# A token mixer whose attention is laid between the matmuls of its input projection

## The chip, the cores and the metric

The kernel runs on one core of one Trainium2 chip. The metric is the device time of one execution in microseconds (us). TensorE (PE), VectorE (DVE), ScalarE (ACT), GpSimd (POOL) and SyncE (SP) each take their own queue of instructions in order, and wait for one another by semaphores. SP issues nearly all DMAs; its transfers follow one another on one ring.

## The reference

The input is x, 256 tokens of 1024 values in float32. A first block has two layers, and each layer is three stages: a gated feed-forward net (FFN1), a token mixer, and a second feed-forward net (FFN2). Each stage is modulated by rows that come from `cond @ w_ada[l] + b_ada[l]`, and each ends in a layer norm. A second block follows: attention with pooling, experts, a short convolution, and experts again; nothing in it is touched here.

The token mixer is where the change is:

```python
def _token_mixer(h, w_in, w_out):
    proj = h @ w_in                          # 1024 -> 3072 columns
    rq, rk, rv, rg, dq, dk, dv, sq, sk, sv = jnp.split(proj, points, axis=-1)
    y_ret = _retention(_rotate(rq), _rotate(rk), rv, rg)   # silu(g) * group_norm(o)
    y_dil = _dilated_attention(_rotate(dq), _rotate(dk), dv)
    y_sb = _stick_breaking(sq, sk, sv)
    return jnp.concatenate([y_ret, y_dil, y_sb], -1) @ w_out
```

(`_split_heads`, `_merge_heads` and the frequencies are left out.) There are four heads of each of the three kinds. All of them read only their own columns of `proj`.

## The kernel before, in words

**The projection.** The 3072 columns are six groups of 512: group 0 is retention q and k, 1 retention v, 2 the gate g, 3 dilated q and k, 4 dilated v and stick-breaking q, 5 stick-breaking k and v. Each group has two token tiles of 128, so there are twelve products (proj0 to proj11, line 767), each of eight contraction steps into one PSUM bank (4 to 7 in turn). ACT copies each bank into `proj` (line 1186). Groups are computed in the order 0 to 5.

**The attention.** After the twelve products PE transposes q and k of all heads (line 789, six sets of four), ACT and DVE copy them out (lines 1199, 1599), and six blocks of two heads follow, in the order `ATT`: dilated, stick-breaking, dilated, stick-breaking, retention, retention. A block is scores (A, lines 799 to 803), a middle part on DVE and ACT, a second PE step (B, lines 813 to 819; not for retention) and the product with the values (C, lines 839 to 841). PE runs two blocks in turn, in banks 4 and 5, and 6 and 7. The gate goes through Silu on ACT (line 1191) ahead of the attention. At the end DVE norms the retention output (lines 1702 to 1714), multiplies it by the gate (line 1718), PE turns y (line 669), and the output projection runs (line 744), first token tile, then second; norm and modulation of the next stage follow on DVE and ACT.

**The modulation rows.** Beside this the kernel computes the rows that later stages need. In the mixer these are five rows a layer, each from a 1024 by 1024 matrix that SP streams into two buffers (`W_mod`) in four chunks of 1 MB (line 407). A chunk's transfer is issued only when DVE has used the chunk two before it. DVE multiplies and adds the chunks (`mod_blocks`, lines 1375 and 1377, eight instructions a row), PE sums over the partitions (`mod_sum`, line 656), DVE adds the bias (line 1391), ACT sends the row to DRAM (line 1088). PE takes the five sums between the products: behind proj2, 4, 6, 8 and 11. DVE takes the rows in one piece each, with the two rotations (lines 1560 to 1566) between them.

**The order of SP's ring.** `MIX_CHUNKS` says ahead of which weight slot which chunks are issued. Weights of `w_in` (slots u = 0 to 11, 1 MB each, line 477), then `w_out` (four of 1 MB), then the first weights of FFN2 follow in the same ring, behind the chunks that stand ahead of them.

All these orders are written out by hand; no planner sets them.

Of the kernel before, what the change touches and what calls it, by code (L numbers as in the profile page):

```python
# [22 lines left out]
P = 128  # L23
S = 256
# [36 lines left out]
MIX_SUMS = (2, 4, 6, 8, 11)  # L61
MIX_CHUNKS = {2: (0, 2), 6: (2, 10), 8: (10, 14), 10: (14, 18), 12: (18, 20)}
# [79 lines left out]
def build(nc, A, out):  # L142
    with ExitStack() as ctx:
# [6 lines left out]
        def steps(name, names):  # L150
            return Steps(sem(name), names)
# [30 lines left out]
        mix_acc = [mod_acc, att_0]  # L182
# [28 lines left out]
        def carve(at, *shape):  # L211
# [116 lines left out]
        m_pe = steps("mixer_pe", [f"proj{n}" for n in range(12)] + [f"qk{g}" for g in range(6)] + ["A0", "A1"]  # L328
                     + sum([([f"B{b}"] if b < 4 else []) + [f"C{b}"] + ([f"A{b + 2}"] if b < 4 else [])
                            for b in range(6)], []) + ["out"])  # L330
        m_act = steps("mixer_act", [f"ev{n}" for n in range(12)] + ["silu_g", "qk0", "qk2", "qk4", "exp0", "ln1",
                                    "PT0", "exp2", "a1", "PT2", "ln3", "a3", "gn_sqrt"])
        m_dve = steps("mixer_dve", ["rot0", "rot1", "qk1", "qk3", "qk5", "max0", "na1", "p0", "lk1", "max2", "y0",
                                    "s1", "am1", "p2", "na3", "y1", "lk3", "y2", "s3", "r4", "am3", "r5", "y3",
                                    "gn_var", "y"])
# [46 lines left out]
        def _(sp):  # L382
# [55 lines left out]
            def ffn_stream(l, k):  # L438
# [4 lines left out]
                if k == 1:  # L443
                    sp.wait_ge(m_pe.s, m_pe.at("out", l))
# [7 lines left out]
            for l in range(LAYERS):  # L452
# [5 lines left out]
                for u in range(MIX_USES):  # L458
# [3 lines left out]
                    if u < 2:  # L462
                        sp.wait_ge(pn_x, l * 6 + 2)
                    elif u < 6:
                        sp.wait_ge(pe_down, l * (2 * TILES) + (1 + TILES))
                    elif s >= 6:
                        last = u - 6 if u < MIX_IN_USES else s
                        sp.wait_ge(m_pe.s, m_pe.at(f"proj{2 * (last // 2) + 1}", l))
                    if u < MIX_IN_USES:
                        g, half = u // 2, u % 2  # L470
# [73 lines left out]
        def _(pool):  # L544
# [85 lines left out]
        def _(pe):  # L630
# [104 lines left out]
            def times_rows(src, slots):  # L735

                at = []
                for tt in range(TT):
# [8 lines left out]
                    if tt == 0:  # L747
                        ins.then_inc(acc_t0, 1)
                return ins

            def mixer(l):
# [7 lines left out]
                for g in range(6):  # L759
                    for t in range(TT):  # L760
                        n = 2 * g + t
                        if n >= 4:
                            pe.wait_ge(m_act.s, m_act.at(f"ev{n - 4}", l))
                        for kc in range(KC):
                            u = 2 * g + kc // 4
                            s = slot(u) if kc % 4 == 0 else MIX_S[u]
                            ins = pe.matmul(psum[:, 4 + n % 4, :], uT[:, kc, P * t:P * t + P],  # L767
                                            part(W[:, s, :], 0, 4, 512)[:, kc % 4, :], start=(kc == 0), stop=(kc == KC - 1))
                        ins.then_inc(m_pe.sig(f"proj{n}"), 1)
                        if n in MIX_SUMS:  # L770
                            row = MIX_SUMS.index(n)
                            mod_sum(l * JOBS_LAYER + (FIRST_JOBS + PAIRS + row), 0, mix_acc[row % 2])

                for g in range(6):
                    kind, hb = g // 2, g % 2
                    if g < 4:
                        pe.wait_ge(m_act.s, m_act.at(f"ev{8 + g}", l))
                    if g == 0:
                        pe.wait_ge(m_dve.s, m_dve.at("rot0", l))
                    if g == 2:  # L780
                        pe.wait_ge(m_dve.s, m_dve.at("rot1", l))
                    if g == 4:
                        pe.wait_ge(m_act.s, m_act.at("qk0", l))
                        pe.wait_ge(m_act.s, m_act.at("ev11", l))
                    if g == 5:
                        pe.wait_ge(m_dve.s, m_dve.at("qk1", l))
                    for n, col in enumerate((QCOL[kind], KCOL[kind])):
                        for t in range(TT):
                            ins = pe.transpose(psum[:, 4 + g % 4, S * n + P * t:S * n + P * t + P],
# [54 lines left out]
                for g in (2, 4):  # L844
                    pe.wait_ge(m_act.s, m_act.at(f"qk{g}", l))
                pe.wait_ge(m_dve.s, m_dve.at("qk5", l))
                scores(0)
                scores(1)
                for b in range(6):
                    if b < 4:  # L850
                        second(b)
                    if b == 4:
                        pe.wait_ge(mod_taken, l * JOBS_LAYER + (FIRST_JOBS + 2 * PAIRS))
                    if b == 2:
                        pe.wait_ge(m_dve.s, m_dve.at("y0", l))
                    if b == 3:
                        pe.wait_ge(m_dve.s, m_dve.at("y1", l))
                    values(b)
                    if b < 4:
                        if ATT[b][0] == STB:  # L860
                            pe.wait_ge(m_dve.s, m_dve.at(f"s{b}", l))
                        scores(b + 2)
# [219 lines left out]
        def _(act):  # L1082
# [100 lines left out]
            def mixer(l):  # L1183
                for n in range(12):
                    act.wait_ge(m_pe.s, m_pe.at(f"proj{n}", l))
                    act.activation(proj[:, n % 2, 512 * (n // 2):512 * (n // 2) + 512], psum[:, 4 + n % 4, :], copy
                                   ).then_inc(m_act.sig(f"ev{n}"), 1)
                    if n in (5, 7, 9):
                        mod_row(l * JOBS_LAYER + (FIRST_JOBS + PAIRS + (n - 5) // 2))
                act.drain()  # L1190
                act.activation(proj[:, :, RG:RG + 512], proj[:, :, RG:RG + 512], ACT.Silu).then_inc(m_act.sig("silu_g"), 1)
                mod_row(l * JOBS_LAYER + (FIRST_JOBS + PAIRS + 3))
                for g in (0, 2, 4):
                    kind, hb = g // 2, g % 2
                    bk = psum[:, 4 + g % 4, :]
# [5 lines left out]
                mod_row(l * JOBS_LAYER + (FIRST_JOBS + PAIRS + 4))  # L1201
# [23 lines left out]

                exps(0)
                logs(1)
                p_turned(0)
                exps(2)
                stick(1)  # L1230
                p_turned(2)
                logs(3)
                stick(3)
                act.wait_ge(m_dve.s, m_dve.at("gn_var", l))
# [731 lines left out]
```

## Time and profile before

| | us |
|---|---|
| median of 3 runs | 2592.54 (2589.14 to 2592.95) |
| the profiled execution, its own time | 2593.06 |
| its span, first to last instruction | 2591.2 |
| PE busy in the span | 2089.6 (81%) |
| DVE busy | 1119.6 (43%) |
| ACT busy | 526.0 (20%) |
| mixer of layer 0, first projection matmul to the turning of y | 251.44 to 410.89 |
| mixer of layer 1, the same | 873.01 to 1031.23 |

A time in the trace is the start of an instruction or of a merged run of them, in us from the start of the span. Of two figures at a row's head the second is how long it lasts.

### The profile page before, as it was taken

What the parts mean: (1) busy time and instruction counts of PE and PEld (TensorE: products, weight loads), DVE (VectorE), ACT (ScalarE), POOL (GpSimd) and SP (SyncE); (2) the same over time, 40 slices, a digit from 0 to 9 for tenths busy, and PEclk for the clock granted to TensorE, in tenths of its full rate; (3) what the DMA queues carried; (4) which work ended last, traced back from release to release, by engine and by line L of the source; (5) the groups of instructions that cost most, each with busy time, mean ns of one, the idle gap of its engine ahead of it and who ended that gap; (6) DMA issues with size and microseconds to landing.
All of it is one profiled execution on the core that took longest, in us unless ns stands there. A gap on an engine that the chain in (4) does not pass through costs nothing.

```text
span 2591.2 us, 33380 instructions
## 1 busy us (share of the span) xinstructions
PE 2089.6 (81%) x12372; PEld 1323.1 (51%) x12372; DVE 1119.6 (43%) x1724; ACT 526.0 (20%) x858; POOL 66.1 (3%) x96
## 2 busy tenths in 40 slices
PE   6998977999799885899978777777769876666664
PEld 4997344999799434599855422222228542111111
DVE  3887554888788665688633310000022331000002
ACT  3332031433334104233323100000010110000000
POOL 1000000000000000000100000000000000000000
PEclk7998987999899898899989787777769978888887
DMA  9986851888588691588721699999995469999996
GB/s 333 327 308 221 290 210 55 281 316 314 201 296 298 212 355 50 187 297 318 268 108 66 235 410 410 410 410 410 410 386 176 167 247 409 410 410 410 410 410 262
DMA packets 289371, 758.03 MB, mean 293 GB/s; under 512 B 17616, under 2 KB 125424, under 8 KB 289184
## 3 DMA queue, kind: packets, MB, share of 16 engines
q1 hardware_dynamic: 282368, 737.34, 75.7%
q0 software_dynamic: 6688, 19.78, 2.4%
q8 instruction: 36, 0.59, 0.1%
q14 instruction: 23, 0.19, 0.0%
q10 hardware_dynamic: 256, 0.13, 0.0%
HBM read 756.01 MB, written 1.18 MB: 292 GB/s over the span
## 4 chain that ended last, share of the span: by engine, by line
PE 51%; DMA 21%; SPq 13%; DVE 8%; issue 3%; ACT 3%; DVEq 1%; ACTq 0%
PE psum L704 20%; DMA W<-in_w_exp_up 15%; SPq L502 12%; PE psum L716 9%; PE psum L744 4%; DMA W_mod<-in_mod_w 4%; PE psum L1071 3%; PE psum L1010 3%; PE psum L767 2%; DMA W<-in_w_exp_down 1%; PE psum L912 1%; PE psum L677 1%; ACT uT L1117 1%; SPq L506 1%; DVE att L1377 1%
## 5 line engine op out<-in xcount | busy, mean ns | idle before, releaser
L704 PE MATMUL psum<-parts 128*128 128x256 f32 x4224 | 528.3, 286 | 14.8 <-DVE parts L1501 7.5
L704 PEld LDWEIGHTS psum<-parts 128*128 128x128 f32 x4224 | 525.8, 195 | 22.4 <-issue 16.2
L1010 PE MATMUL psum<-W,scr 128*32 128x512 f32 x2048 | 316.9, 730 | 151.4 <-DMA W<-in_w_exp_up 136.4
L1877 DVE TENSOR_TENSOR scr<-scr,psum 128x256 f32<-128x256 f32 x32 | 13.5, 421 | 572.4 <-ACT scr L1327 572.4
L1377 DVE SCALAR_TENSOR_TENSOR mod_acc<-W_mod,cond,mod_acc 128x1024 f32<-128x1024 f32 x182 | 233.8, 1285 | 60.1 <-DMA W_mod<-in_mod_w 29.2
L716 PE MATMUL psum<-parts 128*128 128x512 f32 x1056 | 257.8, 393 | 0.0
L1010 PEld LDWEIGHTS psum<-W,scr 128*32 128x32 f32 x2048 | 53.7, 118 | 393.1 <-DMA W<-in_w_exp_up 306.8
L1035 PE MATMUL psum<-W,scr 128*32 128x256 f32 x2048 | 181.3, 498 | 68.3 <-DMA W<-in_w_exp_down 53.2
L1501 DVE TENSOR_TENSOR parts<-W,parts 128x1024 fp32r<-128x1024 f32 x176 | 207.1, 1220 | 56.9 <-ACT parts L1147 56.7
L716 PEld LDWEIGHTS psum<-parts 128*128 128x128 f32 x1056 | 192.6, 188 | 45.3 <-DVE parts L1514 8.2
L1147 ACT ACTIVATE parts<-W 128x1024 fp32r<-128x1024 f32 x176 | 175.7, 1051 | 46.4 <-issue 46.4
L767 PE MATMUL psum<-W,uT 128*128 128x512 f32 x384 | 176.2, 619 | 5.1 <-DVE uT L1421 3.3
L1047 PE MATMUL psum<-scr 128*128 128x512 f32 x256 | 141.8, 704 | 31.9 <-DVE scr L1890 29.8
L1035 PEld LDWEIGHTS psum<-W,scr 128*32 128x32 f32 x2048 | 69.3, 136 | 174.9 <-DMA W<-in_w_exp_down 103.1
L1890 DVE COPY scr<-psum 32x256 f32<-32x256 f32 x64 | 27.2, 426 | 254.8 <-PE psum L1035 254.3
L1327 ACT ACTIVATE scr<-psum 128x256 f32<-128x256 f32 x32 | 12.3, 383 | 603.6 <-PE psum L1010 603.6
L767 PEld LDWEIGHTS psum<-W,uT 128*128 128x128 f32 x384 | 75.3, 199 | 102.4 <-issue 102.4
L1514 DVE TENSOR_TENSOR parts<-W,parts 128x1024 fp32r<-128x1024 f32 x88 | 107.3, 1219 | 10.3 <-ACT parts L1159 10.3
L1166 ACT ACTIVATE att<-psum 128x256 f32<-128x256 f32 x88 | 33.8, 384 | 380.5 <-PE psum L704 380.5
L1047 PEld LDWEIGHTS psum<-scr 128*128 128x128 f32 x256 | 55.0, 227 | 107.6 <-issue 60.4
L1159 ACT ACTIVATE parts<-W 128x1024 fp32r<-128x1024 f32 x88 | 92.9, 1056 | 43.1 <-PE psum L716 43.1
L677 PE MATMUL psum<-k_ident,x_tok 128*128 128x128 f32 x160 | 35.4, 396 | 66.7 <-DVE x_tok L1485 62.2
(283 smaller groups left out, 1744.1 us busy)
## 6 DMA issues: line engine op xcount, KB each, us to landing
W<-in_w_exp_down SPq DMA_DIRECT2D x128, 1024.0 KB
W<-in_w_exp_gate SPq DMA_DIRECT2D x256, 512.0 KB, 14.3
W<-in_w_exp_up SPq DMA_DIRECT2D x256, 512.0 KB, 15.7
W_mod<-in_mod_w SPq DMA_DIRECT2D x123, 1024.0 KB, 6.0
W<-in_ffn_w_gate SPq DMA_DIRECT2D x44, 1024.0 KB, 9.6
W<-in_ffn_w_up SPq DMA_DIRECT2D x44, 1024.0 KB, 12.0
W<-in_ffn_w_down SPq DMA_DIRECT2D x44, 1024.0 KB, 9.3
W<-in_w_in SPq DMA_DIRECT2D x24, 1024.0 KB, 8.5
```

What stands on the lines that cost most here:

```text
L502: sp.dma_start(W[:, s, D * n:D * n + D], w[layer, ds(e, 1), P * s:P * s + P, :] .rearrange("a p n -> p (a n)")).then_inc(landed[s], 16)
L704: ins = pe.matmul(psum[:, 4 + t % 2, S * g:S * g + S], w[:, t % 2, g, kc, :], u[:, kc, :], start=(n == 0 and kc == 0), stop=(n == 2 and kc ...
L716: ins = pe.matmul(psum[:, 2 * tt + h, :], h_[:, t % 2, P * tt:P * tt + P], w[:, t % 2, 512 * h:512 * h + 512], start=(t == 0 and n == 0), ...
L744: ins = pe.matmul(psum[:, 2 * tt + h, :], src[:, kc, P * tt:P * tt + P], w[:, kc % 2, 512 * h:512 * h + 512], start=(kc == 0), stop=(kc == ...
L767: ins = pe.matmul(psum[:, 4 + n % 4, :], uT[:, kc, P * t:P * t + P], part(W[:, s, :], 0, 4, 512)[:, kc % 4, :], start=(kc == 0), stop=(kc ...
L1010: ins = pe.matmul(psum[32 * q:32 * q + 32, 4, :].rearrange("p (g n) -> p g n", g=2), xe_now[:, kc, :], w[:, :, q, :], start=(kc == 0), sto ...
L1035: ins = pe.matmul(psum[32 * q:32 * q + 32, 6, 0:256], e_hT[:, c % 2, 32 * (c // 2):32 * (c // 2) + 32], part(W[:, s, :], 0, 2, D)[:, c % 2 ...
L1047: ins = pe.matmul(psum[:, 2 * tt + h, :], GT[:, P * tt:P * tt + P], R[:, 512 * h:512 * h + 512], start=first, stop=True, skip_group_check= ...
L1147: ins = act.activation(gu_hi[:, t % 2, g, :, :], part(W[:, b + g, :], 0, KC, STEP)[:, :, P * (t % 2):P * (t % 2) + P], copy)
L1377: ins = dve.scalar_tensor_tensor(acc[:, :], w, col, acc[:, :], mul, add)
L1501: ins = dve.tensor_tensor(gu_lo[:, t % 2, g, :, :], part(W[:, b + g, :], 0, KC, STEP)[:, :, P * (t % 2):P * (t % 2) + P], gu_hi[:, t % 2, ...
L1514: dve.tensor_tensor(d_lo[:, t % 2, :], part(W[:, b + 2, :], 0, 2, D)[:, t % 2, :], d_hi[:, t % 2, :].bitcast(F32), sub).then_inc(lo_d, 1)
```

## The change

The order of the groups becomes 3, 4, 5, 0, 1, 2. The products are now called p30, p31, p40 and so on (group, token tile), and the attention's steps stand between them in PE's queue. ACT's and DVE's queues are written in an order that follows. Further:

- Row 3 of the modulation is cut in four pairs of blocks between the attention's steps on DVE; row 4 is computed behind the turning of y, its PE sum stands between the two token tiles of the output projection (a new hook in `times_rows`), its last two chunks are issued with FFN2's stream, and its last steps on DVE (`mixer_row(l, 4)`) and ACT stand in the next norm.
- `MIX_CHUNKS` puts fewer chunks ahead of each weight slot.
- The rotations use `gate_row` as scratch; POOL's load of `gate_row` therefore waits for the second rotation (`rot0`), and the loads behind it in POOL's queue too.
- Probabilities of the dilated heads are turned into columns of the gate (`RG`), and the gate's own product for the second token tile (p21) and the Silu come behind the attention.

The diff, cut to its core:

```diff
-MIX_SUMS = (2, 4, 6, 8, 11)
-MIX_CHUNKS = {2: (0, 2), 6: (2, 10), 8: (10, 14), 10: (14, 18), 12: (18, 20)}
+MIX_GROUPS = (3, 4, 5, 0, 1, 2)
+MIX_BANK = (3, 3, 3, 1, 6)
+MIX_CHUNKS = {2: (0, 2), 6: (2, 8), 8: (8, 12), 10: (12, 16), 12: (16, 18)}
-        mix_acc = [mod_acc, att_0]
+        mix_acc = [mod_acc, att_0, mod_acc, mod_acc, mod_acc]
-        dil_pT = proj[:, :, 0:3 * P]
+        dil_pT = proj[:, :, RG:RG + 3 * P]
-        rope_a, rope_b = tmp[:, 0, 0:512], tmp[:, 1, 0:512]
+        rope_a, rope_b = gate_row[:, 0:512], gate_row[:, 512:1024]
@@ SP, ffn_stream
                 if k == 1:
+                    for c in (2, 3):
+                        mod_chunk(l * JOBS_LAYER + (FIRST_JOBS + 2 * PAIRS - 1), c, PAIRS - 1)
                     sp.wait_ge(m_pe.s, m_pe.at("out", l))
@@ SP, w_in
-                        sp.wait_ge(m_pe.s, m_pe.at(f"proj{2 * (last // 2) + 1}", l))
+                        sp.wait_ge(m_pe.s, m_pe.at(f"p{MIX_GROUPS[last // 2]}1", l))
@@ POOL, gate
+                if s in (1, 4):
+                    pool.wait_ge(m_dve.s, m_dve.at("rot0", s // 3))
@@ PE, times_rows
                     if tt == 0:
                         ins.then_inc(acc_t0, 1)
+                        between()
@@ PE, mixer
+                project(3, 0, 4)
+                project(3, 1, 5)
+                project(4, 0, 6)
+                row_sum(0)
+                project(4, 1, 7)
+                pe.wait_ge(m_act.s, m_act.at("ev30", l))
+                project(5, 0, 4)
+                row_sum(1)
+                pe.wait_ge(m_act.s, m_act.at("ev40", l))
+                pe.wait_ge(m_dve.s, m_dve.at("rot1", l))
+                heads_turned(2, 6)
+                pe.wait_ge(m_act.s, m_act.at("ev31", l))
+                project(5, 1, 5)
+                pe.wait_ge(m_act.s, m_act.at("ev41", l))
+                heads_turned(3, 7)
+                project(0, 0, 0)
+                row_sum(2)
+                pe.wait_ge(m_act.s, m_act.at("ev51", l))
+                heads_turned(4, 6)
+                pe.wait_ge(m_dve.s, m_dve.at("qk3", l))
+                heads_turned(5, 7)
+                scores(0)
+                project(0, 1, 1)
...
+                scores(1)
+                second(0)
...
+                project(1, 0, 0)
+                values(0)
+                scores(2)
+                second(1)
...
+                project(1, 1, 1)
...
+                values(1)
+                scores(3)
+                second(2)
...
+                project(2, 0, 0)
+                pe.wait_ge(m_dve.s, m_dve.at("y0", l))
+                values(2)
+                pe.wait_ge(m_dve.s, m_dve.at("rot0", l))
+                heads_turned(0, 4)
+                heads_turned(1, 5)
...
+                row_sum(3)
+                second(3)
...
+                scores(4)
...
+                values(3)
+                scores(5)
...
+                values(4)
+                values(5)
+                project(2, 1, 4)
                 turn(y_tok, lambda t: (m_dve.s, m_dve.at("y", l)))
                 turned(l * 4 + 2)
-                times_rows(uT, lambda u: slot(MIX_IN_USES + u)).then_inc(m_pe.sig("out"), 1)
+                times_rows(uT, lambda u: slot(MIX_IN_USES + u), lambda: row_sum(4)).then_inc(m_pe.sig("out"), 1)
@@ ACT, mixer (its end)
+                evacuate(2, 0, 0)
+                heads(0, 4)
                 stick(3)
+                row_out(3)
                 act.wait_ge(m_dve.s, m_dve.at("gn_var", l))
                 act.activation(rstd[:, :], rstd[:, :], ACT.Sqrt).then_inc(m_act.sig("gn_sqrt"), 1)
+                evacuate(2, 1, 4)
+                act.drain()
+                act.activation(proj[:, :, RG:RG + 512], proj[:, :, RG:RG + 512], ACT.Silu).then_inc(m_act.sig("silu_g"), 1)
                 turn(l * 4 + 2)
@@ DVE, mixer
+                mixer_blocks(0)
+                rotated(1, DIL, 3)
+                mixer_blocks(1)
+                mixer_row(l, 0)
+                mixer_blocks(2)
+                mixer_row(l, 1)
+                heads(3, 7)
+                mixer_blocks(3, 0, 2)
+                mixer_row(l, 2)
+                heads(5, 7)
                 maxima(0)
+                mixer_blocks(3, 2, 4)
+                weighted(0)
                 neg_abs(1)
-                weighted(0)
+                rotated(0, RET, 0)
                 keeps(1)
+                mixer_blocks(3, 4, 6)
                 maxima(2)
+                sticks(1)
                 dil_out(0)
-                sticks(1)
                 stick_mask(1)
                 weighted(2)
+                stick_out(1)
                 neg_abs(3)
-                stick_out(1)
+                mixer_blocks(3, 6, 8)
                 keeps(3)
                 dil_out(2)
+                heads(1, 5)
+                mixer_row(l, 3)
                 sticks(3)
                 decayed(4)
                 stick_mask(3)
...
                 turn(l * 4 + 2)
+                mixer_blocks(4)
@@ DVE, between the mixer and its norm
                 plus_bias(s + 1)
+                mixer_row(l, 4)
```

## Rows read from the trace of the kernel before

**Rows 1.** The chain that ended last, from the page: by engine, by line.

```profile
PE 51%; DMA 21%; SPq 13%; DVE 8%; issue 3%; ACT 3%; DVEq 1%; ACTq 0%
PE psum L704 20%; DMA W<-in_w_exp_up 15%; SPq L502 12%; PE psum L716 9%; PE psum L744 4%; DMA W_mod<-in_mod_w 4%; PE psum L1071 3%; PE psum L1010 3%; PE psum L767 2%; DMA W<-in_w_exp_down 1%; PE psum L912 1%; PE psum L677 1%; ACT uT L1117 1%; SPq L506 1%; DVE att L1377 1%
```

**Rows 2.** Timeline of PE, layer 0's mixer: start, us, line, what, count, idle before.

```profile
251.44 23.91 PE L767 MATMUL psum<-W,uT 128*128 128x512 f32 x48 [1.67 <-DVE uT L1421]
...
291.24 14.00 PE L767 MATMUL psum<-W,uT 128*128 128x512 f32 x32
...
325.61 0.88 PE L656 MATMUL psum<-att,k_ones 128*32 128x256 f32 x8 [3.90 <-DVE mod_out L1391]
326.42 22.27 PE L767 MATMUL psum<-W,uT 128*128 128x512 f32 x48
348.63 0.64 PE L656 MATMUL psum<-mod_acc,k_ones 128*32 128x256 f32 x8
349.20 1.97 PE L789 MATMUL psum<-k_ident,scr 128*128 128x128 f32 x16
...
362.19 0.88 PE L813 MATMUL psum<-k_ident,att 128*128 128x128 f32 x6 [3.91 <-DVE att L1624]
...
403.27 0.39 PE L841 MATMUL psum<-scr,tmp 128*128 128x128 f32 x2
410.89 3.68 PE L669 MATMUL psum<-k_ident,tmp 128*128 128x128 f32 x16 [7.24 <-DVE tmp L1718]
415.46 27.70 PE L744 MATMUL psum<-W,uT 128*128 128x512 f32 x64 [0.90 <-issue]
```

**Rows 3.** Windows: stretch, length, busy us of five engines, granted clock, DMA.

```profile
290.00:349.00 59.00, 52.70 (x144) 22.22 (x144) 34.84 (x39) 4.33 (x8) 3.53 (x4) 0.97 0.95 348
349.00:362.00 13.00, 6.11 (x48) 5.07 (x40) 8.89 (x23) 9.42 (x19) 0.00 (x0) 1.00 0.82 284
362.00:404.00 42.00, 28.22 (x132) 24.01 (x132) 18.68 (x48) 13.75 (x16) 0.00 (x0) 0.72 0.00 0
```

**Rows 4.** Timeline of PE, layer 1's mixer: beginning, end of the projection, turning of y.

```profile
873.01 23.73 PE L767 MATMUL psum<-W,uT 128*128 128x512 f32 x48 [1.66 <-DVE uT L1421]
...
970.64 1.97 PE L789 MATMUL psum<-k_ident,scr 128*128 128x128 f32 x16
...
1031.23 3.68 PE L669 MATMUL psum<-k_ident,tmp 128*128 128x128 f32 x16 [7.41 <-DVE tmp L1718]
```

**Rows 5.** Timeline of DVE, layer 0: modulation rows, first softmax, the next norm.

```profile
299.09 5.38 DVE L1377 SCALAR_TENSOR_TENSOR mod_acc<-W_mod,cond,mod_acc 128x1024 f32<-128x1024 f32 x4 [3.81 <-DMA W_mod<-in_mod_w]
304.39 0.42 DVE L1391 TENSOR_TENSOR mod_out<-psum,cond_now 128x256 f32<-128x256 f32 x1
...
357.01 0.42 DVE L1612 SCALAR_TENSOR_TENSOR att<-psum,k_closed 128x256 f32<-128x256 f32 x1 [1.40 <-PE psum L800]
...
429.47 1.23 DVE L1462 TENSOR_TENSOR tmp<-psum,gate_row 128x1024 f32<-128x1024 f32 x1 [5.91 <-PE psum L744]
...
443.21 1.23 DVE L1462 TENSOR_TENSOR tmp<-psum,gate_row 128x1024 f32<-128x1024 f32 x1 [9.34 <-PE psum L744]
```

**Rows 6.** Timeline of SP: DMA issues, layer 0's mixer.

```profile
286.07 1.02 SPq L477 DMA_DIRECT2D W<-in_w_in  x2
...
304.91 1.08 SPq L477 DMA_DIRECT2D W<-in_w_in  x2
```

**Rows 7.** DMA issues of 236 to 456 us: KB each, us to landing.

```profile
W_mod<-in_mod_w SPq DMA_DIRECT2D x20, 1024.0 KB, 6.2
W<-in_w_in SPq DMA_DIRECT2D x10, 1024.0 KB, 8.8
```

**Rows 8.** Timeline of ACT: the gate's Silu in layer 0.

```profile
348.73 0.60 ACT L1186 ACTIVATE scr<-psum 128x512 f32<-128x512 f32 x1 [6.27 <-PE psum L767]
349.39 1.28 ACT L1191 ACT_TABLE_LOAD   x1
350.69 1.06 ACT L1191 ACTIVATE scr<-scr 128x1024 f32<-128x1024 f32 x1
```

More of the change, by code:

```diff
@@ L326, in build @@
         s_out = sem("out_stored")
[L328 to L335, printed above, removed]
+        m_pe = steps("mixer_pe", "p30 p31 p40 p41 p50 qk2 p51 qk3 p00 qk4 qk5 A0 p01 A1 B0 p10 C0 A2 B1 p11 C1 A3 B2 p20 C2 "
+                     "qk0 qk1 B3 A4 C3 A5 C4 C5 p21 out".split())
+        m_act = steps("mixer_act", "ev30 ev31 ev40 ev41 ev50 qk2 ev51 ev00 qk4 exp0 ev01 ln1 PT0 ev10 exp2 a1 ev11 PT2 ln3 "
+                      "ev20 qk0 a3 gn_sqrt ev21 silu_g".split())
+        m_dve = steps("mixer_dve", "rot1 qk3 qk5 max0 p0 na1 rot0 lk1 max2 s1 y0 am1 p2 y1 na3 lk3 y2 qk1 s3 r4 am3 r5 y3 "
+                      "gn_var y".split())
         P2 = [f"c{t}" for t in range(TT)] + [f"p{t}{g}" for t in range(TT) for g in range(3)]
@@ L733, in ffn, with times_rows @@
                 pe.wait_ge(mod_taken, l * JOBS_LAYER + (FIRST_JOBS + PAIRS + 2 * PAIRS * k))
-            def times_rows(src, slots):
+            def times_rows(src, slots, between=lambda: None):
                 at = []
@@ L756, in slot @@
                     return s
[L759 to L772, printed above, removed]
@@ L774, in mixer, with project @@
-                for g in range(6):
-                    kind, hb = g // 2, g % 2
[L776 to L786, printed above, removed]
+                def project(g, t, bank):
+                    for kc in range(KC):
+                        u = 2 * MIX_GROUPS.index(g) + kc // 4
+                        s = slot(u) if kc % 4 == 0 else MIX_S[u]
+                        ins = pe.matmul(psum[:, bank, :], uT[:, kc, P * t:P * t + P],
+                                        part(W[:, s, :], 0, 4, 512)[:, kc % 4, :], start=(kc == 0), stop=(kc == KC - 1))
+                    ins.then_inc(m_pe.sig(f"p{g}{t}"), 1)
@@ L846, in mixer @@
+                pe.wait_ge(m_act.s, m_act.at("qk4", l))
                 pe.wait_ge(m_dve.s, m_dve.at("qk5", l))
-                scores(0)
                 scores(1)
[L849 to L862, printed above, removed]
+                second(0)
@@ L1183, in mixer, with evacuate, row_out, heads @@
             def mixer(l):
[L1184 to L1193, printed above, removed]
+                def evacuate(g, t, bank):
+                    act.wait_ge(m_pe.s, m_pe.at(f"p{g}{t}", l))
+                    act.activation(proj[:, t, 512 * g:512 * g + 512], psum[:, bank, :], copy).then_inc(m_act.sig(f"ev{g}{t}"), 1)
+                def row_out(n):
+                    mod_row(l * JOBS_LAYER + (FIRST_JOBS + PAIRS + n))
+                def heads(g, bank):
                     kind, hb = g // 2, g % 2
-                    bk = psum[:, 4 + g % 4, :]
+                    bk = psum[:, bank, :]
                     act.wait_ge(m_pe.s, m_pe.at(f"qk{g}", l))
@@ L1567, in rotate, with mixer_row, mixer_blocks, heads @@
                 ins.then_inc(m_dve.sig(f"rot{table}"), 1)
+            def mixer_row(l, n):
+                job = l * JOBS_LAYER + (FIRST_JOBS + PAIRS + n)
+                mod_row(job, (pe_mod, job - FIRST_JOBS + 2), MIX_BANK[n], None, mix_bias[n % 2], 2 * l + (n + 1) // 2)
             def mixer(l):
-                def mixer_blocks(n):
+                def mixer_blocks(n, first=0, end=KC):
                     job = l * JOBS_LAYER + (FIRST_JOBS + PAIRS + n)
-                    mod_blocks(job, job - FIRST_JOBS - (1 if n else 0), 0, KC, mix_acc[n % 2])
-                def mixer_row(n):
-                    job = l * JOBS_LAYER + (FIRST_JOBS + PAIRS + n)
-                    mod_row(job, (pe_mod, job - FIRST_JOBS + 2), 0, None, mix_bias[n % 2], 2 * l + (n + 1) // 2)
+                    mod_blocks(job, job - FIRST_JOBS - (1 if n in (1, 2) else 0), first, end, mix_acc[n])
                 def rotated(table, kind, group):
                     dve.drain()
-                    dve.wait_ge(m_act.s, m_act.at(f"ev{2 * group + 1}", l))
+                    dve.wait_ge(m_act.s, m_act.at(f"ev{group}1", l))
                     rotate(l, kind, table)
-                mixer_blocks(0)
-                mixer_blocks(1)
-                rotated(0, RET, 0)
-                mixer_row(0)
-                mixer_blocks(2)
-                mixer_row(1)
-                mixer_blocks(3)
-                mixer_row(2)
-                rotated(1, DIL, 3)
-                mixer_blocks(4)
-                mixer_row(3)
-                for g in (1, 3, 5):
+                def heads(g, bank):
                     kind, hb = g // 2, g % 2
-                    bk = psum[:, 4 + g % 4, :]
+                    bk = psum[:, bank, :]
                     dve.wait_ge(m_pe.s, m_pe.at(f"qk{g}", l))
```

38 lines of the change are left out of this document (32 added, 6 removed).

## The prediction

> **What bounds the kernel now.** I read the chain that ended last first [rows 1]: TensorE holds 51% of it, and the DMAs that hold 21% and most of SP's 13% belong to the experts' weights, which the change does not touch. The feed-forward nets around each mixer are lines 704 and 716, 29% of the chain, so a mixer that ends earlier moves all that follows it by the same amount. Then PE's timeline in layer 0's mixer [rows 2]. The twelve products run from 251.44 to 349.20, nearly without a gap. The attention follows to 403.66. The norm of the retention heads and the gate's multiplication take until 410.89, where y is turned; the output projection starts at 415.46. The reader is to see two unlike halves in the windows [rows 3]. From 290 to 349 PE is busy 52.70 of 59 us and ACT 4.33. From 349 to 404 PE is busy 6.11 + 28.22 of 55 us, and the second part of that runs at a granted clock of 0.72. PE waits there for short steps of DVE and ACT that hang on one another. Layer 1 has the same form, 873.01 to 1031.23 [rows 4]: 158.2 us against 159.5.
>
> **What a product costs.** 32 records of line 767 last from 291.24 to 305.17, two products, so 6.9 us each [rows 2]. The first three took 23.91 us where 3 x 6.9 = 20.7: 3.2 us lost to the low clock at the start. The attention's own PE work at full clock is 6.11 x 1.00 + 28.22 x 0.72 = 26.4 us [rows 3], the turning of q and k included. A row's sum costs 0.6 us [rows 2].
>
> **PE's new queue, layer 0.** Up to the last values (C5) it holds eleven products, 75.9 us; the slow start, 3.2; four sums, 2.4; the attention, 26.4. That is 107.9 us. Nothing of the arithmetic goes; what goes is the idle time of the attention, into which seven products (p51 to p21) are laid. Before, the same point was reached after 403.66 - 251.44 = 152.2 us.
>
> **The waits that stay.** First, the third row's sum. PE gets there after seven products, two sums, the slow start and two sets of turned heads (1.0): 53.7 us, at 305.1. DVE had the second row done at 304.8 before [rows 5], paced by `W_mod`: a chunk lands 6.2 us after its issue [rows 7] and is issued only when DVE has used the one two before. In the new ring two slots of w_in (2 MB) pass ahead of chunks 8 and 9, where they came behind them at 286.07 [rows 6]; at the ring's 348 to 400 GB/s that is 2.6 us a MB, half of it hidden behind the two-chunk loop, so row 2 is ready near 307.5. The rotation stays one, in another gap. Wait: 2.4 us, between 0 and 5. Second, the first dilated block. Chunk 12 lands behind slots 8 and 9 of w_in, near 312 (before, these slots came at 304.91, behind chunk 13). Behind it DVE does two blocks (2.6), a row (0.4), a head group (1.3, three copies of the size of line 1391's), the maxima, two more blocks (2.6) and the weighting. From the start of the maxima to B0 it was 5.2 us before (357.01 to 362.19 [rows 2, 5]), of which 1.9 is the stick-breaking step that now comes later; so B0 is free near 312 + 4.3 + 3.3 + 2.6 = 322.2. PE is there at 319: 307.5 plus a sum, two sets of heads, a product and two scores. Wait: 3.2 us, between 0 and 6. Third, the values of block 3: two decay products and two mask products on DVE, 0.42 for 256 columns [rows 5], about 2 us with nothing of PE's ahead. All other steps of DVE and ACT lie beside a product of 6.9 us, which is longer than the logarithms' chain with its table load. These three waits are 7.6 us. A gap also costs clock: behind a wait of 3.90 us a sum took 0.88 and three products 22.27 instead of 20.7 [rows 2], 1.6 to 1.8 us. I take 2.5 for gaps of this size, between 0 and 5. C5 ends after 107.9 + 7.6 + 2.5 = 118.0 us.
>
> **The end of the mixer.** Before, 7.2 us stood between C5 and the turning [rows 2]. Now the product p21 is behind C5 (6.9), and the gate comes behind it: the copy 0.60, the table load 1.28, the Silu 1.06 [rows 8], the multiplication 1.23 (the size of line 1462's [rows 5]), with 0.3 between them: 11.4 us. The norm of the retention heads hides under p21. The Silu was free before, beside the turning of q and k; here it is the last link. The copy needs no table of its own, and the load stood right behind the copy in the row, 0.06 us after it, so I do not let it start before p21.
>
> Here a rule of the Trainium skill and the row differ. In the row the Silu starts 0.02 us after the load's 1.28 have passed [rows 8]. The Trainium skill (ScalarE: Activation LUTs, What ACT_TABLE_LOAD costs) adds a drain of about 1.38 us to every switch, 2.66 in all. By that the two layers together would be 2.8 us later. The measured row decides, and the sum goes without it.
>
> **The sum.** y is turned after 118.0 + 11.4 = 129.4 us instead of 159.5: 30.1 us less in layer 0. In layer 1, 158.2 - 129.4 = 28.8. Off this comes the output projection's added sum, 0.6 a layer. Row 4 now starts on DVE only behind the turning of y. Its eight blocks take 10 us, and its last two chunks (issue to landing 6.2 us [rows 7]) bring it to about 13.8; the first token tile ends 14.0 us after the projection's start (415.46 to 429.47 [rows 2, 5]). So PE just does not wait, or up to 3 us if a chunk takes the 8.8 us of w_in [rows 7]. DVE then has two splits of gate and up weights, the bias, the row and the first half of the norm, 13 us, and is free at 27; the second half of the norm was late on PE at 27.8 (443.21). The cover is about one us thick; I take 0.3 a layer. POOL's load of gate_row and the columns behind it come some 70 us later than before and are needed only in the next norm, 100 us further on: nothing. w_out is issued behind chunk 17, near 348, and lands by 366; it is needed at 382: nothing. Together 30.1 + 28.8 - 1.2 - 0.6 = 57.1. Against the profiled execution's own 2593.06 this gives 2535.9; that run stands 0.5 above the median of 2592.54. I say 2535.
>
> **The range.** With none of the waits and no clock loss each layer gives 10.1 more: 2515. With the waits at their upper ends (5, 6, 4), 5 of clock and 3 in the output projection, 13 less: 2561. For eight in ten I take 2516 to 2553.
>
> **Rivals.** (a) DVE and the `W_mod` loop set the pace. For it: DVE was busy 62.4 of the 114 us from 290 to 404 [rows 3], and the same work, less row 4's 10 us, must fit a stretch 34 us shorter, in a strict order with blocks that wait for DMA (3.81 us before one group [rows 5]). Against it: after chunk 13 every block has its data long before its turn. If each of the seven interleaved steps waited 3 us, 21 instead of 7.6, two layers would give 27 less: 2562. Chance 0.10. (b) The clock stays low in the whole interleaved stretch. For it: 0.72 in 362 to 404, where PE worked in short pieces [rows 3]. Against it: 0.97 from 290 to 349 with gaps up to 3.90 us. Place: p51 to p21 with the attention, 7 x 6.9 + 26.4 = 74.7 us at full clock. At the lower of the two levels, 1.2 of 2.4 GHz, it costs 74.7 a layer against 29 gained: 2593 + 2 x 46 = 2685. It turns to slower where the mean clock is under 74.7 / (74.7 + 29) = 0.72. Chance 0.03. The Trainium skill (TensorE: Matmul & The Clock Gate, A second HAM failure mode: psum-queue depth-cycling) speaks against this change: short pauses between groups of matmuls can make the clock swing between its two levels. The gap rows show that only in part, 1.7 us behind a gap of 3.90. (c) The gain is won and mostly given back in the output stage, because row 4 is late: chunks 18 and 19 queue behind FFN2's first 3 MB, and norm and PE slip by 8 us a layer: 2551. Those 3 MB should be in before; chance 0.05. (d) The change does not do what it says, a wait in PE's queue (the count of `mod_taken`, or `ev` of a late bank) holds the products until the old times: 2593. PE's order makes that unlikely; 0.02. The forecast itself has 0.80.
>
> A measurement here tells 0.2%, 5 us, from no change. All of (a), (c) and the forecast are faster by more; so faster is 0.95; same is (d), 0.02; slower is (b), 0.03.
>
> **What would show it.** In the trace after: y turned near 129 us after the first product; the idle time before the third sum, before B0 and before block 3's values 2 to 3 us each; granted clock above 0.9 from 290 to 370; the table load of the Silu behind the copy of p21 and 4 to 5 us of idle PE there; the sum of row 4 without idle before it, and the second half of the norm still released by PE. A clock near 0.7, or DVE waiting for `W_mod` behind chunk 13, or more than 15 us of idle PE between the first product and C5, would make it wrong.

## The result, and the profile after

The changed kernel takes 2526.37 us (median of 4 runs, 2524.13 to 2532.63) beside 2590.84 for the kernel before on the same chip (2588.03 to 2592.95, 4 runs). The ratio is 0.9756, 95% interval 0.9735 to 0.9777: 2.4% faster. Predicted were 2535.0, between 2516 and 2553. The profiled execution took 2525.63, its span is 2523.8 (before: 2591.2), so 67.4 us less.

The page after, the chain that ended last, by engine and by line (answers to [rows 1]):

```profile
PE 54%; DMA 21%; SPq 13%; DVE 6%; issue 3%; ACT 2%; DVEq 1%; ACTq 0%
PE psum L707 20%; DMA W<-in_w_exp_up 16%; SPq L503 12%; PE psum L719 9%; PE psum L747 5%; PE psum L768 4%; PE psum L1103 3%; DMA W_mod<-in_mod_w 3%; PE psum L1042 3%; DMA W<-in_w_exp_down 1%; PE psum L944 1%; PE psum L680 1%; SPq L507 1%; ACT uT L1149 1%; PE psum L1054 1%
```

The shares of the experts' weights are nearly as they were. PE has more of the chain, DVE and ACT less, and the products (now line 768) went from 2% to 4%: they bridge what was a chain through DVE and ACT.

PE's timeline in layer 0's mixer after, the first products, the rows with a wait, the products that stand between steps, and the turning of y (answers to [rows 2]):

```profile
249.58 23.40 PE L768 MATMUL psum<-W,uT 128*128 128x512 f32 x48 [1.66 <-DVE uT L1476]
...
304.24 0.64 PE L659 MATMUL psum<-mod_acc,k_ones 128*32 128x256 f32 x8 [1.42 <-DVE mod_out L1446]
...
307.15 7.03 PE L768 MATMUL psum<-W,uT 128*128 128x512 f32 x16
...
318.69 0.87 PE L805 MATMUL psum<-k_ident,att 128*128 128x128 f32 x6 [3.20 <-DVE att L1668]
319.40 8.73 PE L768 MATMUL psum<-W,uT 128*128 128x512 f32 x16
...
332.35 7.03 PE L768 MATMUL psum<-W,uT 128*128 128x512 f32 x16
...
342.52 7.03 PE L768 MATMUL psum<-W,uT 128*128 128x512 f32 x16
...
357.39 0.41 PE L831 MATMUL psum<-scr,tmp 128*128 128x64 f32 x2 [1.87 <-DVE tmp L1693]
...
362.84 7.03 PE L768 MATMUL psum<-W,uT 128*128 128x512 f32 x16
374.23 3.60 PE L672 MATMUL psum<-k_ident,tmp 128*128 128x128 f32 x16 [4.36 <-DVE tmp L1778]
```

From 307 on four products stand 10 to 13 us apart, with steps of the attention between them, and p21, the last product, starts at 362.84. From the first product to C5 only three gaps are left in front of PE: the third row's sum, the first dilated block's turning (B0), the values of block 3 (C3). All other steps of the attention find their input ready. Layer 1 begins and its y is turned here (answers to [rows 4]):

```profile
836.18 23.64 PE L768 MATMUL psum<-W,uT 128*128 128x512 f32 x48 [1.66 <-DVE uT L1476]
...
961.82 3.36 PE L672 MATMUL psum<-k_ident,tmp 128*128 128x128 f32 x16 [4.36 <-DVE tmp L1778]
```

The mixer, from its first product to the turning of y, is 124.65 us in layer 0 (before 159.45) and 125.64 in layer 1 (before 158.22): 34.8 + 32.6 = 67.4 us. That is all of the span's gain. Of the other stretches, the one before layer 0's mixer is 1.9 shorter, the one between the mixers 0.2 shorter, and the one behind layer 1's turning 2.0 longer.

The windows of the same places after, columns as in [rows 3]: 290 to 349, then 290 to 363 (C5), then up to the turning:

```profile
290.00:349.00 59.00, 54.38 (x189) 29.26 (x188) 43.96 (x77) 17.93 (x27) 4.05 (x5) 0.97 0.62 218
290.00:363.00 73.00, 66.51 (x278) 39.68 (x277) 51.49 (x96) 22.96 (x34) 4.05 (x5) 0.98 0.70 254
363.00:374.00 11.00, 6.87 (x16) 2.69 (x15) 6.39 (x27) 3.15 (x4) 0.00 (x0) 1.00 0.68 232
```

ACT is busy 17.93 us from 290 to 349 where it was 4.33, and the stretch at a clock of 0.72 [rows 3] is gone: 0.98 up to C5.

### The profile page after: what moved, and what is told of

Read it like the earlier page. It is cut to its first block, busy times and chain, and to the rows that moved or that the text cites. A ratio compares the mean times of both kernels' runs of the same rounds, so it can differ in the third digit from the quotient of the medians.

```text
span 2523.8 us, 33380 instructions
## 1 busy us (share of the span) xinstructions
PE 2078.4 (82%) x12372; PEld 1309.9 (52%) x12372; DVE 1118.6 (44%) x1724; ACT 528.9 (21%) x860; POOL 65.2 (3%) x96
## 4 chain that ended last, share of the span: by engine, by line
PE 54%; DMA 21%; SPq 13%; DVE 6%; issue 3%; ACT 2%; DVEq 1%; ACTq 0%
PE psum L707 20%; DMA W<-in_w_exp_up 16%; SPq L503 12%; PE psum L719 9%; PE psum L747 5%; PE psum L768 4%; PE psum L1103 3%; DMA W_mod<-in_mod_w 3%; PE psum L1042 3%; DMA W<-in_w_exp_down 1%; PE psum L944 1%; PE psum L680 1%; SPq L507 1%; ACT uT L1149 1%; PE psum L1054 1%
## 5 line engine op out<-in xcount | busy, mean ns | idle before, releaser
L1042 PE MATMUL psum<-W,scr 128*32 128x512 f32 x2048 | 323.7, 743 | 136.3 <-DMA W<-in_w_exp_up 122.9
L1432 DVE SCALAR_TENSOR_TENSOR mod_acc<-W_mod,cond,mod_acc 128x1024 f32<-128x1024 f32 x196 | 251.8, 1284 | 51.6 <-issue 28.2
L1556 DVE TENSOR_TENSOR parts<-W,parts 128x1024 fp32r<-128x1024 f32 x176 | 207.0, 1219 | 56.1 <-ACT parts L1179 56.1
L1067 PE MATMUL psum<-W,scr 128*32 128x256 f32 x2048 | 165.8, 463 | 73.6 <-DMA W<-in_w_exp_down 58.5
L1079 PE MATMUL psum<-scr 128*128 128x512 f32 x256 | 160.1, 782 | 31.7 <-DVE scr L1952 29.7
L768 PE MATMUL psum<-W,uT 128*128 128x512 f32 x384 | 176.6, 617 | 3.3 <-DVE uT L1476 3.3
L1079 PEld LDWEIGHTS psum<-scr 128*128 128x128 f32 x256 | 63.3, 262 | 117.7 <-issue 70.3
L1569 DVE TENSOR_TENSOR parts<-W,parts 128x1024 fp32r<-128x1024 f32 x88 | 107.2, 1218 | 10.3 <-ACT parts L1191 10.3
L747 PE MATMUL psum<-W,uT 128*128 128x512 f32 x192 | 86.6, 611 | 2.7 <-issue 1.9
```

Of the source, the lines that this page charges most:

```text
L747: ins = pe.matmul(psum[:, 2 * tt + h, :], src[:, kc, P * tt:P * tt + P], w[:, kc % 2, 512 * h:512 * h + 512], start=(kc == 0), stop=(kc == ...
L768: ins = pe.matmul(psum[:, bank, :], uT[:, kc, P * t:P * t + P], part(W[:, s, :], 0, 4, 512)[:, kc % 4, :], start=(kc == 0), stop=(kc == KC ...
L1042: ins = pe.matmul(psum[32 * q:32 * q + 32, 4, :].rearrange("p (g n) -> p g n", g=2), xe_now[:, kc, :], w[:, :, q, :], start=(kc == 0), sto ...
L1067: ins = pe.matmul(psum[32 * q:32 * q + 32, 6, 0:256], e_hT[:, c % 2, 32 * (c // 2):32 * (c // 2) + 32], part(W[:, s, :], 0, 2, D)[:, c % 2 ...
L1079: ins = pe.matmul(psum[:, 2 * tt + h, :], GT[:, P * tt:P * tt + P], R[:, 512 * h:512 * h + 512], start=first, stop=True, skip_group_check= ...
L1432: ins = dve.scalar_tensor_tensor(acc[:, :], w, col, acc[:, :], mul, add)
```

## Experiments

All ratios are to the kernel before, run on the same chip; "mixer" is first product to turning of y, layer 0 / layer 1, in the profiled execution.

**1. The attention behind all products.** Order of the column groups, rows and ring (but one chunk) as changed; only the interleaving is undone, on PE and in ACT's copies.

```diff
- ... qk5 A0 p01 A1 B0 p10 C0 A2 B1 p11 C1 A3 B2 p20 C2 qk0 qk1 B3 A4 C3 A5 C4 C5 p21
+ ... qk5 p01 p10 p11 p20 p21 A0 A1 B0 C0 A2 B1 C1 A3 B2 C2 qk0 qk1 B3 A4 C3 A5 C4 C5
```

> The changed kernel with its order of groups, its rows and its rings, but the attention again behind all twelve products: p01, p10, p11, p20 and p21 stand ahead of the first scores (the last two stay in banks 0 and 1 until the second dilated block is done, and the ring gives slots 10 and 11 one chunk earlier). Theory (the gain is idle time of the attention that the products fill): the first scores begin 5 x 6.9 = 34 us later than after, and from them to the last values it takes the 48 us of before, plus up to 5 us for the row's blocks that DVE has between; the end of the mixer is 7 us again, since the gate is ready. So 22 to 30 us more a layer: 2570 to 2586, idle PE of about 20 us back in each attention, granted clock there near 0.75. Rival (the order of the groups and the modulation rows moved behind bring it): at most 10 us a layer more, 2546 or less.

Measured: 2573.43 us, ratio 0.9919 [0.9901, 0.9936]; mixer 151.63 / 152.02, 27.0 and 26.4 above the changed kernel, inside the 22 to 30 expected. Windows of its products' second half and of its attention:

```profile
308.00:341.60 33.60, 33.60 (x82) 14.95 (x81) 3.54 (x6) 3.95 (x7) 0.00 (x0) 1.00 0.41 154
342.50:396.00 53.50, 35.27 (x165) 29.48 (x163) 36.65 (x78) 18.03 (x26) 4.06 (x5) 0.71 0.51 176
```

The two unlike halves are back: first PE alone at full clock, then DVE busy 36.65 of 53.50 us and a clock of 0.71. So the interleaving itself is worth 53.4 of the 67.4 us, in the mixers of the profiled executions; the medians of this run and the changed kernel are 47.1 us apart. PE's marked waits inside the mixer add up to 27.0 us in layer 0 here and to 10.9 in the changed kernel, so 16.1 of the 27.0 us are idle time. Nearly all of the other 10.9 is the same matmuls at a lower clock: two scores of line 794 take 0.59 us at 343.72 and 1.17 at 369.65. The other 7.8 us of layer 0 are mostly in the products' stretch. It ran 97.8 us before (251.44 to 349.20 [rows 2]) and 91.0 here. Before, it held waits of 0.83, 1.73 (for `w_in`) and 3.90 us; here it holds one of 1.52:

```profile
306.47 0.64 PE L659 MATMUL psum<-mod_acc,k_ones 128*32 128x256 f32 x8 [1.52 <-DVE mod_out L1441]
308.07 34.50 PE L768 MATMUL psum<-W,uT 128*128 128x512 f32 x80
```

**2. Only the late sum, in the kernel before.** It asks whether that 3.90 us wait alone could have been moved away.

```diff
-MIX_SUMS = (2, 4, 6, 8, 11)
+MIX_SUMS = (2, 4, 6, 9, 11)
```

> The kernel before with one number changed: PE's sum of the fourth row stands behind proj9 instead of proj8, so that PE does not wait for DVE there (3.9 and 4.0 us before, and some 1.7 us of low clock behind the wait in layer 0). Theory (PE's queue bounds the projection, so a wait in it is time in full): 8 to 11 us less, 2580 to 2583. Rival (the chunk loop of the rows bounds the projection, and the wait only moves to the fifth sum): no change, 2588 to 2593.

Measured: 2599.08 us, ratio 1.0017 [1.0005, 1.0028]; mixer 160.58 / 161.70. My theory fell; the rival's number, no change, is right, though the fifth sum does not wait either. The fourth sum waits no more, but PE now reaches the next weights before they are there:

```profile
327.41 0.64 PE L656 MATMUL psum<-att,k_ones 128*32 128x256 f32 x8
331.81 16.77 PE L767 MATMUL psum<-W,uT 128*128 128x512 f32 x32 [3.77 <-DMA W<-in_w_in]
```

Those weights are issued behind a chunk that waits for DVE. The wait changed its name from DVE to DMA, and did not shrink (3.77 us in layer 0 and 5.05 in layer 1, where the sum had waited 3.90 and 4.00): what had to change was the order of the ring and of DVE, not the place of the sum.

**3. Another order of the ring.** Two chunks of row 2 ahead of the weights of the first retention group, as two slots of weights passing ahead of them had been priced at 2.6 us a MB.

```diff
-MIX_CHUNKS = {2: (0, 2), 6: (2, 8), 8: (8, 12), 10: (12, 16), 12: (16, 18)}
+MIX_CHUNKS = {2: (0, 2), 6: (2, 10), 8: (10, 14), 10: (14, 16), 12: (16, 18)}
```

> The changed kernel with another order of SP's ring: chunks 8 and 9 ahead of slots 6 and 7 of w_in, chunks 12 and 13 ahead of slots 8 and 9. Theory (the waits before the third sum, 1.4 and 1.1 us, and before the first B, 3.2 and 4.2 us, come from chunks 8 and 12 that land behind 2 MB of w_in): both waits fall under 1 us, and the product behind B0 takes 6.9 instead of 8.6 us: 5 to 6 us less a layer, 2514 to 2517. Rival (DVE's two blocks between the maxima and the weighting hold B0, not the chunk): 2 us less a layer, 2522. Rival on the other side (w_in is late for p00 or p10 instead): same or slower, 2526 or more.

Measured: 2519.64 us, ratio 0.9721 [0.9700, 0.9741]; mixer 121.80 / 122.25, so 2.85 and 3.4 less, between the theory (5 to 6) and the first rival (2). Its waits and what follows them:

```profile
316.19 0.87 PE L805 MATMUL psum<-k_ident,att 128*128 128x128 f32 x6 [0.98 <-DVE att L1668]
316.90 7.03 PE L768 MATMUL psum<-W,uT 128*128 128x512 f32 x16
...
353.21 0.41 PE L831 MATMUL psum<-scr,tmp 128*128 128x64 f32 x2 [1.87 <-DVE tmp L1693]
...
354.65 1.17 PE L794 MATMUL psum<-qm,scr 128*128 128x256 f32 x2
355.61 0.64 PE L795 MATMUL psum<-qm,scr 128*128 128x128 f32 x2
```

The sum's wait went down by 0.78 and B0's by 2.22, and the product behind B0 is back at 7.03, another 1.7. That would be 4.7. But behind C3's unchanged gap of 1.87 the scores now take 1.17 and 0.64, where after the change they took 0.65 and 0.38, and C3 to the last product takes 7.06 us instead of 5.45. The clock's dip was not removed: it moved, and 1.6 us came back. That is the part of the theory that failed: it had the waits nearly right and counted the dip as gone.

**4. The gate ahead of the last product.** Half of the gate (token tile 0) and the table load are taken before the product p21 is waited for; tile 1 goes through Silu straight from PSUM, and DVE multiplies tile by tile.

```diff
-                evacuate(2, 1, 4)
                 act.drain()
-                act.activation(proj[:, :, RG:RG + 512], proj[:, :, RG:RG + 512], ACT.Silu)...
+                act.activation(proj[:, 0, RG:RG + 512], proj[:, 0, RG:RG + 512], ACT.Silu)...
+                act.wait_ge(m_pe.s, m_pe.at("p21", l))
+                act.activation(proj[:, 1, RG:RG + 512], psum[:, 4, :], ACT.Silu)...
```

> The changed kernel with the gate's end shortened: the Silu of the first token tile, with the table load, stands before p21 is awaited, the second token tile goes through Silu straight from PSUM, and DVE multiplies tile by tile. Theory (after p21 the copy, the table load, the Silu and the multiplication hang on one another, 4.3 us in all): 1.4 us are left, so 2.9 us less a layer, 2520 to 2521. Rival (the norm of the retention heads ends just as late, or a table load costs a drain besides): less than 1 us a layer, 2525 or more.

Measured: 2513.61 us, ratio 0.9687 [0.9667, 0.9708]; mixer 121.74 / 121.97, 2.9 and 3.7 less. ACT's timeline, then the turning of y on PE:

```profile
366.35 1.28 ACT L1288 ACT_TABLE_LOAD   x1
367.64 0.63 ACT L1288 ACTIVATE scr<-scr 128x512 f32<-128x512 f32 x1
370.27 0.60 ACT L1290 ACTIVATE scr<-psum 128x512 f32<-128x512 f32 x1 [2.00 <-PE psum L768]
```

```profile
371.64 1.97 PE L672 MATMUL psum<-k_ident,tmp 128*128 128x128 f32 x16 [1.41 <-DVE tmp L1781]
```

PE's gap fell from 4.36 to 1.41 as expected. The total is 6.4 to 7.4 us below the expectation, and a third of that has a reason that I had not put in. After the change the turning's 16 matmuls ran for 3.60 us behind the gap of 4.36 (3.36 in layer 1); here, behind 1.41, they take 1.97. From the turning to the next net's first matmul it is 43.46 / 43.12 us instead of 44.53 / 44.41, so 2.4 us in all. Layer 1's mixer gives 0.8 beyond the expectation, and there B0's gap is 3.27 instead of 4.22, which the gate does not explain. Where the other 3 to 4 us come from stays open.

**5. Both together, and the changed kernel again.** The edits are those of 3 and 4.

> The changed kernel with both repairs at once: the ring's chunks and weights in the order of the run with the new ring (row chunks 8 and 9 ahead of the weights of the first retention column group), and the gate's Silu and its table load ahead of the last product. The ring's repair took 2.9 and 3.4 us a layer from the mixer (first product to the turning of y) in the stretch up to 350, the gate's 2.9 and 3.7 in the tail, with another 1 us in the output stage: they lie in different places, so theory: they add up, mixer 118.5 to 119.5 a layer against 124.65 and 125.64, span 13 to 17 us below that of the changed kernel, ratio 0.962 to 0.965 of the kernel before. Rival: the tail's gain came from a clock that stays at full speed over the turning of y, and one of the two is used up: then 2512 to 2515, ratio 0.968.

> The changed kernel itself, unaltered, beside the others on the same chip, so that they can be compared with it directly. Ratio to the kernel before 0.974 to 0.978; mixer 124 to 126 us a layer.

Measured: both 2512.67 us, ratio 0.9688 [0.9674, 0.9703], mixer 118.80 / 119.16. The changed kernel 2525.40, ratio 0.9743 [0.9727, 0.9759], mixer 124.49 / 125.29. In the mixer the gains add up as expected: 5.7 and 6.1 a layer below the repetition of the changed kernel. The turning of y takes 1.96 / 1.97 us as in experiment 4, so the rival's cause, a gain that is used up twice, is not seen, although the total lies where the rival put it. The ratio that I expected (0.962 to 0.965) was missed because it did not fit the rest of my expectation: 13 to 17 us below the changed kernel is a ratio of 0.968 to 0.971. Against the repetition on the same chip the medians differ by 12.7 us and the mixers by 11.8, so nothing is missing. What is not told apart from this is the total of experiment 4, 12.8 us below the changed kernel with only 6.6 in its mixers. The profiled execution of both repairs was its fastest, 2505.52, the others took 2510 to 2514. From layer 1's turning of y to the end the profiles of these kernels differ by up to 8 us without a system (1554.3 here, 1562.0 after the change, 1558.5 in its repetition, 1561.1 in experiment 3), and a sum of mixer gains below that size is seen in the mixer only.

**6. The last idle gap filled.** On top of both repairs, the scores A5 stand ahead of C3 on PE, and on DVE the copy behind C3 ahead of the decay of block 5.

```diff
- ... A4 C3 A5 C4 C5 p21        DVE: ... r4 am3 r5 y3
+ ... A4 A5 C3 C4 C5 p21        DVE: ... r4 am3 y3 r5
```

> As the run before it in this list (both repairs), and in addition the scores of the second retention pair of heads ahead of the values of the second stick-breaking pair on TensorE (they wait for the sum that VectorE took of the other pair instead), and on VectorE the copy of the stick-breaking values ahead of the second decay. The idle 1.87 us of TensorE ahead of the values is then filled by scores of 1.3 us, but VectorE's decay comes one copy (some 0.4 us) and one wait later. Theory: 0.3 to 1.3 us a layer less than with both repairs, no more. Rival: the chain from VectorE's mask through values, copy and decay to the last values is as long as what it replaces, and nothing is left (within 0.3 us a layer).

Measured: 2504.51 us, ratio 0.9654 [0.9637, 0.9671]; mixer 116.36 / 116.90, 2.4 and 2.3 less than with both repairs, twice what was expected. PE's timeline:

```profile
353.29 0.60 PE L794 MATMUL psum<-qm,scr 128*128 128x256 f32 x2
353.73 0.38 PE L795 MATMUL psum<-qm,scr 128*128 128x128 f32 x2
354.58 0.43 PE L831 MATMUL psum<-scr,tmp 128*128 128x64 f32 x2 [0.47 <-DVE tmp L1694]
```

The gap is 0.47 instead of 1.87, and the granted clock from 308 to 359 is 1.00:

```profile
308.00:359.00 51.00, 49.57 (x224) 31.49 (x223) 39.55 (x84) 20.73 (x29) 4.06 (x5) 1.00 0.74 274
```

So 1.4 us is the gap and 1.3 the dip, which is seen in neither layer now (C3 to p21 takes 4.44 us, and 7.10 with the scores of 1.31 in it before); 0.3 is lost ahead of it. This version beats both kernels: 3.5% below before, and its interval lies wholly below that of the changed kernel.

**7. Two products fewer between the steps.** In the changed kernel, p01 and p10 stand ahead of the first scores (and their copies ahead on ACT), so that only p11 and p20 are left inside, and p21 in the tail.

```diff
- ... qk5 A0 p01 A1 B0 p10 C0 A2 B1 p11 C1 A3 B2 p20 C2 ...
+ ... qk5 p01 p10 A0 A1 B0 p11 C0 A2 B1 p20 C1 A3 B2 C2 ...
```

> The changed kernel with the attention begun two products later: the second product of group 0 and the first of group 1 stand ahead of the first scores, and three of the five products are left between steps of the attention (the last one stays in the tail). Theory: a product between two steps is worth the wait of VectorE that it covers and the clock that it keeps. Without a product between the first scores and the turning of the first dilated weights, that wait grows from 3.2 us to 8 to 10, and the third dilated step loses its cover as well (some 3 us more), each with a slow product behind it: 8 to 13 us a layer more than the changed kernel, 2542 to 2554. Rival: three products are cover enough, since VectorE is less loaded later on, and the loss is 2 to 4 us a layer: 2530 to 2535.

Measured: 2548.73 us, ratio 0.9833 [0.9814, 0.9852]; mixer 135.95 / 136.20, 11.3 and 10.6 more. The size is as expected, the places only in part:

```profile
329.51 1.54 PE L805 MATMUL psum<-k_ident,att 128*128 128x128 f32 x6 [4.77 <-DVE att L1668]
330.85 7.94 PE L768 MATMUL psum<-W,uT 128*128 128x512 f32 x16
...
360.80 1.65 PE L810 MATMUL psum<-scr,k_later 128*128 128x384 f32 x2 [2.57 <-DVE scr L1693]
```

B0's wait grew to 4.77 (5.12 in layer 1), not to 8: DVE had worked ahead beside the two products and waited for PE's scores before the maxima:

```profile
323.48 0.42 DVE L1656 SCALAR_TENSOR_TENSOR att<-psum,k_closed 128x256 f32<-128x256 f32 x1 [8.31 <-PE psum L792]
```

The rest came late, at the second stick-breaking block (2.57) and behind it, where its large matmuls take 1.65 instead of 0.91 in experiment 6. The clock from 350 to 372 is 0.80, and 1.00 in the changed kernel. In layer 0 PE's waits add up to 6.0 us more than in the changed kernel; the other 5.3 of the 11.3 are nearly all the same matmuls at the lower clock.

## Why the prediction was right, point by point

- **Place and sign.** All of the 67.4 us are in the two mixers, and experiment 1 gives 53.4 of them to the interleaving. Rival (d) is out. The sum of 57.1 is 10.3 short of the span's gain: 8.5 in the two mixers, and 1.8 that I took off for the output stage and that did not come. The mechanism held; most of the errors of size point the same way, so the number was not saved by errors that cancel.
- **PE's queue up to C5.** 107.9 us of work were counted. C5 ended 113.4 after the first product, not 118.0. Of the 4.6, waits are 1.1, the clock's loss 0.8, the slow start 0.5. The rest, 2.2, is the **mis-sized term**: the attention's work, 26.4. What C5's time leaves for it, 113.4 - 75.9 - 2.4 - 2.7 (slow start, 23.40 - 3 x 6.9) - 6.5 (waits) - 1.7 (clock) = 24.2 us. Adding up the attention's rows of the new timeline from start to start, where they run at or near full clock, gives 24.2 as well. I had multiplied PE's busy time by the granted clock [rows 3]. That this came out 2.2 too high may lie in the records, whose ends are modelled and overlap, or in the clock, which is a mean over idle time too; no run separates the two. The product's 6.9 us holds: single ones take 6.87 from start to start, though the pair that I read it from takes 6.97 each.
- **The waits.** The third sum 1.42 / 1.14 (forecast 2.4), B0 3.20 / 4.22 (3.2), C3 1.87 / 1.87 (2.0). This mixer starts 1.9 us earlier than the one before, so its times are compared from the first product: row 2 was done on DVE after 54.5 us (at 304.1), not 56.1, and PE came after 53.2, not 53.7. The chain before B0 came out by its parts, 9.6 us from the chunk's landing to B0 for 10.2 forecast; DVE's first wait there is for the chunk that was named, chunk 12, which lands 59.5 us after the first product (at 309.1), not 60.6:

```profile
309.10 0.75 DVE L1430 TENSOR_SCALAR mod_acc<-W_mod,cond 128x1024 f32<-128x1024 f32 x1 [3.81 <-DMA W_mod<-in_mod_w]
```

- **Clock behind gaps.** One product of 8.73 / 8.44 instead of 7.03, so 1.7 / 1.4 us for 2.5 forecast; in layer 1 the turning at B0 ahead of it loses another 0.3.
- **The tail.** From the end of C5 to the turning 11.2 us for 11.4, link by link: copy, table load, Silu, multiplication (answers to [rows 8]):

```profile
369.90 0.60 ACT L1219 ACTIVATE scr<-psum 128x512 f32<-128x512 f32 x1 [3.98 <-PE psum L768]
370.57 1.28 ACT L1289 ACT_TABLE_LOAD   x1
371.86 1.06 ACT L1289 ACTIVATE scr<-scr 128x1024 f32<-128x1024 f32 x1
```

```profile
372.95 1.23 DVE L1778 TENSOR_TENSOR tmp<-tmp,scr 128x1024 f32<-128x1024 f32 x1 [4.07 <-ACT scr L1289]
```

Here the load is on the path that sets the end, and Silu starts 0.01 us behind its 1.28. The drain that the Trainium skill (ScalarE: Activation LUTs, What ACT_TABLE_LOAD costs) adds to every switch would have put Silu at 373.2. The runs do not show it, and the sum without it held.
- **The output stage.** Row 4's sum stands at 392.63 without idle before it, and DVE waits for PE with the second half of the norm:

```profile
407.23 1.22 DVE L1517 TENSOR_TENSOR tmp<-psum,gate_row 128x1024 f32<-128x1024 f32 x1 [2.76 <-PE psum L747]
```

The cover is 2.76 us thick; one was forecast. From the turning to the next net's first matmul it is 44.53 / 44.41 us, before 44.30 / 45.56. I had added 0.9 a layer, and +0.23 and -1.15 came: rival (c) is out.
- **Rival (a)**, DVE and `W_mod` as pace: two of the three waits do come from there, but they are 4.6 and 5.4 us a layer, and all three together 6.5 and 7.2, not 21. Experiment 7's 11 us are not this rival, since DVE waits for PE there. **Rival (b)**, the clock: 0.98 up to C5, with one dip a layer. In experiment 1's attention the clock is 0.71, and it swings: scores of the same shape take 0.59 us in one place and 1.17 in another. Such a swing in short pauses is what the rule that was put against the change says (the Trainium skill, TensorE: Matmul & The Clock Gate, A second HAM failure mode: psum-queue depth-cycling); the trace of experiment 1 agrees with it, that of the changed kernel hardly shows it.

## What to carry to other kernels

Where one engine waits in a chain of short steps while it also has long independent work, count how much of that work lies inside the chain, not only how much there is: here the five products that experiment 1 moves out were worth 5.3 us each on average (27.0 and 26.4 a layer, the last of the five in the tail), and the two of experiment 7 5.5 each, in idle time and in clock. Price the wait that stays first, then look which gap is next: a wait removed alone can come back under another name (experiment 2), or its clock dip can move to the next gap (experiment 3), and only when the gap of 1.87 us went too did the dip go (experiment 6; gaps of up to 1.21 us before C5 and 1.42 before the turning are left there, and none is followed by a dip). Work that was hidden, like the gate's Silu, must be priced again where it becomes the last link, and split so that its first half and the table load lie beside the last product.

## What the runs showed of the hardware

- **A gap's length does not tell its dip.** In the changed kernel B0's gap of 3.20 us costs 1.7 in the product behind it and C3's of 1.87 nothing. With B0's gap at 0.98 (experiment 3) its product is at full speed and C3's gap costs 1.6. In layer 1 of experiment 4 the gap before B0 is 3.27, yet the product behind it takes 7.03, and the dip stands behind C3. In experiment 7, layer 0, there are three: at B0's turning and product (1.54 and 7.94 behind 4.77), at the second stick-breaking block (1.65 behind 2.57) and at the scores behind C3 (1.17 behind 1.87). From layer 1 of experiment 4:

```profile
902.42 0.87 PE L805 MATMUL psum<-k_ident,att 128*128 128x128 f32 x6 [3.27 <-DVE att L1669]
903.13 7.03 PE L768 MATMUL psum<-W,uT 128*128 128x512 f32 x16
...
941.51 1.02 PE L794 MATMUL psum<-qm,scr 128*128 128x256 f32 x2
```

So a dip can't be put down to the gap before it by that gap's length alone, and there need not be just one; which gap it follows stays open.
- **The price of a dip falls on what stands behind it.** The turning of y, 16 small matmuls, took 3.60 us behind a gap of 4.36 and 1.97 behind 1.41. That is 1.6 us in a stretch for which I had priced no clock at all; before the change the same 16 took 3.68 behind 7.24, so the change itself gained next to nothing there.
